# Sixteen conditioning slabs of the second layer in the first mixer, one for each attention step

## The reference, cut to what matters

```
for li in range(DEPTH):
    mod = c_act @ w_ada[li] + b_ada[li]            # (1, 6 * 1024); mod_c likewise from c_ctx
    sh1, sc1, g1, sh2, sc2, g2 = jnp.split(mod, 6)
    m = unpack(modulate(rms_norm(x, norm1_w[li]), sh1, sc1) @ w_in[li], ...)
    att, rec, four = attention(m), gated_recurrence(m), fourier_mix(m)
    x = x + g1 * (concat(att, rec, four) @ w_out[li])
    x = x + g2 * conv_ffn(modulate(rms_norm(x, norm2_w[li]), sh2, sc2), w_up[li], ..., w_down[li])
```

## Time and profile before

| | us |
|---|---|
| median of 3 runs | 1996.9 |
| lowest, highest | 1995.39, 1999.26 |
| the profiled execution, its span | 1989.8 |
| TensorE matmul, busy | 1816.6 (91%) |
| TensorE weight load, busy | 1524.2 (77%) |
| VectorE, busy | 1081.2 (54%) |
| ScalarE, busy | 849.0 (43%) |

### The profile page before, as it was taken

The page is one execution under the profiler, slowest core; times in us unless marked ns, Lnnn a source line. Parts: engine busy times, 40 slices in busy tenths (PEclk is TensorE's granted clock), DMA queues, the critical chain, the costliest instruction groups (busy, mean ns, idle before and its releaser), DMA issues.

```text
span 1989.8 us, 27657 instructions
## 1 busy us (share of the span) xinstructions
PE 1816.6 (91%) x11308; PEld 1524.2 (77%) x11308; DVE 1081.2 (54%) x1620; ACT 849.0 (43%) x1243; POOL 78.0 (4%) x135
## 2 busy tenths in 40 slices
PE   5999888699999999988988889897999899999888
PEld 3777766577777778876766679877999788988776
DVE  1333477654444464454467658755665655545564
ACT  2342444433333343244344445544343446556542
POOL 0000001210000000010001100001000000000010
PEclk9999989899999999988988889898999999999889
DMA  9653200034455532243210455444666455555541
GB/s 292 218 188 114 79 1 1 1 106 153 154 161 168 169 106 96 75 153 128 85 43 1 132 190 189 148 169 127 191 186 183 163 164 169 169 170 169 133 65 43
DMA packets 211596, 261.34 MB, mean 131 GB/s; under 512 B 4673, under 2 KB 173299, under 8 KB 211215
## 3 DMA queue, kind: packets, MB, share of 16 engines
q1 hardware_dynamic: 207850, 248.28, 38.4%
q0 software_dynamic: 3232, 11.15, 3.0%
q10 hardware_dynamic: 389, 0.15, 0.0%
HBM read 258.43 MB, written 1.12 MB: 130 GB/s over the span
## 4 chain that ended last, share of the span: by engine, by line
PE 74%; DVE 10%; ACT 6%; DMA 5%; issue 3%; SPq 1%; POOL 1%; DVEq 0%; ACTq 0%
PE acc L675 21%; PE acc L677 20%; PE acc L676 20%; DVE weights_low L1822 2%; DMA weights<-in_w_in_dram 2%; PE acc L716 2%; DVE scratch L2009 2%; ACT weights_high L1382 2%; PE acc L928 1%; PE acc L1215 1%; DMA weights<-in_w_up_dram 1%; PE acc L1191 1%; PE acc L1145 1%; SPq L1233 1%; DMA weights<-in_w_down_dram 1%
## 5 line engine op out<-in xcount | busy, mean ns | idle before, releaser
L1822 DVE TENSOR_TENSOR weights_low<-weights,weights_high 128x2048 fp32r<-128x2048 f32 (+1 forms) x184 | 416.8, 2268 | 578.0 <-ACT weights_high L1382 577.8
L1382 ACT ACTIVATE weights_high<-weights 128x2048 fp32r<-128x2048 f32 (+1 forms) x184 | 348.3, 1896 | 644.2 <-DMA weights<-in_w_up_dram 190.7
L675 PE MATMUL acc<-normed_t_high,weights_high 128*128 128x256 f32 (+1 forms) x1824 | 580.9, 318 | 12.8 <-DVE weights_low L1822 11.4
L676 PE MATMUL acc<-normed_t_low,weights_high 128*128 128x256 f32 (+1 forms) x1824 | 567.0, 311 | 0.0
L677 PE MATMUL acc<-normed_t_high,weights_low 128*128 128x256 f32 (+1 forms) x1824 | 566.6, 311 | 0.0
L675 PEld LDWEIGHTS acc<-normed_t_high,weights_high 128*128 128x128 f32 x1824 | 348.7, 191 | 41.2 <-DVE weights_low L1822 14.0
L676 PEld LDWEIGHTS acc<-normed_t_low,weights_high 128*128 128x128 f32 x1824 | 346.6, 190 | 24.0 <-issue 4.3
L677 PEld LDWEIGHTS acc<-normed_t_high,weights_low 128*128 128x128 f32 x1824 | 346.0, 190 | 21.3
L675 PE MATMUL acc<-weights_high,normed_t_high 128*128 128x512 f32 (+1 forms) x792 | 314.6, 397 | 33.2 <-DVE normed_t_low L2178 28.3
L676 PE MATMUL acc<-weights_low,normed_t_high 128*128 128x512 f32 (+1 forms) x792 | 310.0, 391 | 0.0
L677 PE MATMUL acc<-weights_high,normed_t_low 128*128 128x512 f32 (+1 forms) x792 | 309.9, 391 | 0.0
(11 more groups left out here) (235 smaller groups left out, 1846.9 us busy)
## 6 DMA issues: line engine op xcount, KB each, us to landing
weights<-in_w_up_dram SPq DMA_DIRECT2D x44, 1024.0 KB, 7.2
weights<-in_attn_w_in_dram SPq DMA_DIRECT2D x40, 1024.0 KB, 5.1
weights<-in_w_ada_dram SPq DMA_DIRECT2D x38, 1024.0 KB, 5.4
weights<-in_conv_w_in_dram SPq DMA_DIRECT2D x32, 1024.0 KB, 5.7
weights<-in_w_in_dram SPq DMA_DIRECT2D x24, 1024.0 KB, 7.3
weights<-in_w_down_dram SPq DMA_DIRECT2D x20, 1024.0 KB, 5.0
arena<-in_w_ada_dram SPq DMA_DIRECT2D x8, 1024.0 KB, 9.9
weights<-in_w_out_dram SPq DMA_DIRECT2D x8, 1024.0 KB, 5.0
```

The lines of the kernel that those rows point to most:

```text
L675: pe.matmul(o, ah, bh, start=start, stop=False)
L676: pe.matmul(o, ah, bl, start=False, stop=False)
L1382: act.activation(hi_slot(n)[:, 0:used], slot(n)[:, 0:used], ACT.Copy).then_inc(hi_in.sem, 1)
L1822: dve.tensor_tensor(slot(n, ring_lo)[:, 0:used], slot(n)[:, 0:used], hi_slot(n)[:, 0:used], ALU.subtract).then_inc(lo_in.sem, 1)
```

## The change

Sixteen slabs of layer 1 leave the `w_up` stage of layer 0 and form a stage ("mixer", 0), one for each of the attention steps 0 to 15. In `plan` they stand between `w_in` and `w_out`. They use one row buffer, `mixer_row`; it was the home of the squares of the head norm, which go to the high slot of the first `w_out` item in layer 0 (`squares_to`). That item is therefore no longer split before the mixer: `split_to` in `w_in` ends one item earlier, and a `split_next` is written at step U + 2 = 18 of ScalarE's `attention` and of VectorE's `combine`. The hunks in order: names, `FILL` and its readers, `row_of`, `plan`, `squares_to`, TensorE's `attention`, ScalarE's `w_in` and `attention`, VectorE's `w_in` and `combine`.

```diff
--- before.py
+++ after.py
@@ -276,6 +276,7 @@
         AT = arena[:, 6144:7168].rearrange("p (b n) -> p b n", b=2)
         ON = ht_r[:, 3080:3336].rearrange("p (b n) -> p b n", b=2)
         o_squares = ht_r[:, 3336:3592].rearrange("p (b n) -> p b n", b=2)
+        mixer_row = ht_r[:, 3336:3592]
         wo_t = scr[:, 0:1024].rearrange("p (b n) -> p b n", b=2)
         START_HOME = [*(arena[:, SLOT * n:SLOT * (n + 1)] for n in range(6)), ht_b[:, 0:SLOT], ht_b[:, SLOT:2 * SLOT]]
         EXTRA = {(0, 18): 4, (0, 19): 8}
@@ -472,13 +473,14 @@
 
         FILL = {"start": ([(0, n) for n in range(8)], [1] * 8),
                 ("w_in", 0): ([(0, n) for n in range(8, 18)], [1] * 10),
-                ("w_up", 0): ([(0, n) for n in range(20, 24)] + [(1, n) for n in (*range(8), *range(12, 20))], [1] * 20),
+                ("mixer", 0): ([(1, n) for n in (*range(8), *range(12, 20))], [1] * 16),
+                ("w_up", 0): ([(0, n) for n in range(20, 24)], [1] * 4),
                 ("w_in", 1): ([(1, n) for n in range(8, 12)], [0, 0, 1, 1, 1, 1]),
                 ("w_up", 1): ([(1, n) for n in range(20, 24)], [1] * 4)}
 
         def fill(stage, n):
 
-            slots, each = FILL[stage]
+            slots, each = FILL.get(stage, ([], []))
             return slots[sum(each[:n]):sum(each[:n + 1])]
 
         def spread(stage, lj):
@@ -488,8 +490,8 @@
 
         def last_spread(stage, n):
 
-            slots, each = FILL[stage]
-            return slots[-1:] if n == len(each) - 1 else []
+            slots, each = FILL.get(stage, ([], []))
+            return slots[-1:] if each and n == len(each) - 1 else []
 
         def first_item(N):
 
@@ -503,6 +505,8 @@
 
             if (li, n) in FILL["start"][0]:
                 return start_rows[:, n, :]
+            if (li, n) in FILL["mixer", 0][0]:
+                return mixer_row
             return extra_rows[:, n % 2, :] if (li, n) in EXTRA else grow[:, ADA_NO[li, n] % 2, :]
 
         def plan_ada(li, n):
@@ -519,6 +523,9 @@
                 else:
                     by_columns(("w_in", li, name, h), W, c0)
                 for lj in fill(("w_in", li), n):
+                    plan_ada(*lj)
+            for n in range(len(att_units(li))):
+                for lj in fill(("mixer", li), n):
                     plan_ada(*lj)
             for c in range(2):
                 for h in range(2):
@@ -573,6 +580,10 @@
 
         def hi_slot(n):
             return ring_hi[:, nth_split[n] % HIGH * SLOT:(nth_split[n] % HIGH + 1) * SLOT]
+
+        def squares_to(li, u):
+
+            return hi_slot(item[("w_out", li, 0, 0)])[:, u % 2 * P:(u % 2 + 1) * P] if li == 0 else o_squares[:, u % 2, :]
 
         def gate_part(li, m):
 
@@ -1000,6 +1011,12 @@
                             r = slice(64 * c, 64 * c + 64)
                             pe.matmul(o[:, 0:nk_], QA[r, h, cols_of(t)], KA[r, h, 0:nk_], start=True, stop=True).then_inc(full, 1)
                     yield
+                    for lj in last_spread(("mixer", li), st - 1):
+                        ada_spread(*lj)
+                    for lj in fill(("mixer", li), st):
+                        for before in spread(("mixer", li), lj):
+                            ada_spread(*before)
+                        ada(*lj)
                     if 0 <= st - 1 < U:
                         u = st - 1
                         t, h = au[u]
@@ -1499,7 +1516,7 @@
                     for lj, at_ in EXTRA.items():
                         if li == 0 and n == at_:
                             ada(*lj)
-                    split_to(min(last_item(("w_in", li, name, h), ("w_in", li), n) + SLOTS, item[("w_out", li, 0, 0)] + 2 - 2))
+                    split_to(min(last_item(("w_in", li, name, h), ("w_in", li), n) + SLOTS, item[("w_out", li, 0, 0)] - (li == 0)))
                 act.wait_ge(full, full_after(("qh", li, 1)))
                 gate_exp(li, 0)
                 gate_high(li, 0)
@@ -1630,7 +1647,7 @@
                         b = slice(u % 2, u % 2 + 1)
                         if u >= 2:
                             act.wait_ge(o_rs.sem, o_rs.after((li, u - 2)))
-                        act.activation(o_squares[:, u % 2, :], bank(("av", li, u), P), ACT.Square,
+                        act.activation(squares_to(li, u), bank(("av", li, u), P), ACT.Square,
                                        scale=arec[:, u % 3, 0:1], accum_out=ossq[:, b]).then_inc(o_sq.sem, 1)
                         act.activation(ON[:, u % 2, :], bank(("av", li, u), P), ACT.Copy, scale=arec[:, u % 3, 0:1]).then_inc(taken_of(("av", li, u)), 1)
                     if 0 <= st - 3 < U:
@@ -1639,6 +1656,11 @@
                         act.wait_ge(full, full_after(("oT", li, u)))
                         act.activation(MT[:, h, cols_of(t)], bank(("oT", li, u), P), ACT.Copy,
                                                            scale=pcol(("subln", li))).then_inc(taken_of(("oT", li, u)), 1)
+                    for lj in fill(("mixer", li), st):
+                        ada(*lj)
+                    if li == 0 and st == U + 2:
+                        act.wait_ge(o_rs.sem, o_rs.after((li, U - 1)))
+                        split_next()
                     yield
 
             def split_rows(X, key, n, r0, nrow, lo, last_read=None):
@@ -2129,6 +2151,13 @@
                         dve.wait_ge(*taken_after(("av", li, u)))
                         dve.tensor_scalar(ON[:, b, :], ON[:, b, :], orstd[:, b:b + 1],
                                                               1.0 - lam_init, ALU.mult, ALU.mult).then_inc(o_done.sem, 1)
+                    for lj in fill(("mixer", li), st):
+                        for before in spread(("mixer", li), lj):
+                            ada(*before)
+                    for lj in last_spread(("mixer", li), st - 1):
+                        ada(*lj)
+                    if li == 0 and st == U + 2:
+                        split_next()
                     yield
 
             def attention(li):
```

## The result

Before: 1996.9 us (median of 7 runs, 1988.1 to 2002.7). After: **2011.6 us** (7 runs, 2005.1 to 2024.1). The ratio is **1.0079**, 95% interval 1.0055 to 1.0104: slower by 11 to 21 us. The forecast was 2008.2, range 1997.5 to 2015.5, with 0.76 for slower. The profiled execution of after has a span of 2007.9 us, against 1989.8: 18.1 us more.

The account below looks back on a forecast made before the run. TensorE bounds the up-projection; the mixer is a ring of small steps around VectorE. Removal -26.2, mixer +18.5, split +7.0, lag +8.5, clock +3.5 sum to +11.3 us, giving 2008.2 us, range 1997.5 to 2015.5.

Parts of the forecast that it names:

- The removal: First up-projection: taking out the sixteen slabs and their spreads saves 26.2 us, all on the path.
- The mixer: First mixer: the slabs moved into its ring of small steps lengthen it by 18.5 us.
- The tail: Mixer steps 14 to 18: the slabs find TensorE idle there and cost 1 us.
- the even steps: Mixer: scores wait for a bank until VectorE's late addition of the spread, delaying the mask; 9.2 us.
- the odd steps: Mixer units 1 to 7: slab ahead of aT delays TensorE's chain to the next s; 8.3 us together.
- The split: First w_out item: VectorE splits it only after the mixer, so TensorE's first w_out matmul comes 7.0 us later.
- The lag: Start of w_up: VectorE stays one split behind, so the first w_up item is split after the norm; 8.5 us later.
- the clock: After the idle gaps before w_out and w_up TensorE restarts at a lower clock; 1.1 and 2.4, together 3.5 us.
- The gaps take it all: Rival: TensorE's idle time in the mixer absorbs the slabs, mixer grows by 3 us; 1992.7 us, chance 0.12.
- The clock stays up: Rival: slabs keep TensorE at 2.4 GHz in the mixer, saving some 5 us; 2003.2 us, chance 0.17.
- The ring pays more: Rival: slabs cost the mixer the upper bound of 28 us instead of 18.5; 2017.7 us, chance 0.14.
- The split does run: Rival: VectorE's w_out split runs inside the mixer, first gap 1.5 us, second none; 1990.7 us, chance 0.03.

Follow-up runs that it names:

- (8): Two kernels against the kernel before: eight slabs in odd or even mixer steps only, eight left in the up-projection, early w_out split; odd 0.9973, even 1.0024.
- the kernel with the lag alone: Kernel before, no slab moved, VectorE's list of splits ending one item earlier in the first w_in; ratio to the kernel before 1.0109, 21.7 us more.
- run 14: Not a label of a run: the text says that from 415.70 to 421.71 us 14 matmuls run, with run as a verb.
- experiment 4: Changed kernel with VectorE's addition of a spread put first in its even combine steps; ratio to the kernel before 1.0067, 2.4 us less than the changed kernel.
- experiment 1: Changed kernel with VectorE's missing first w_out split put right behind the weave; ratio to the kernel before 1.0000, 15.8 us less than the changed kernel.
- the kernel with both edits: Changed kernel with VectorE's w_out split behind the weave and its spread addition first in even steps; ratio to the kernel before 0.9933, then 0.9958.

## Why the forecast held, step by step

**The removal** (-26.2): right, a little low; the kernel without slabs takes 27.2 us less there. The gate spread of slab (0, 23), for which I had kept back 1.0 us, is still there (eight matmuls of L727 at 500.10 us), so some other part of that sum is 1.0 us too low; which is open.

**The mixer** (+18.5, and 1.4 of the split's 7.0 ahead of the rows, together 19.9): the profile shows +23.9. The mean of more executions is nearer to the forecast. The first mask of unit 7 is at 353.40, 355.42 and 360.81 in three executions of the old ring (mean 356.5), and at 373.48, 372.67, 368.62 and 379.77 in four with sixteen slabs and the addition last (mean 373.6): **+17.1** up to there, against 17.5 forecast. The tail from that mask to the rows grew from 31.3 to 35.1, 3.8 us against 1 and 1.4: too small by 1.4. So the sum was right while its split was not: the even steps pay some three times what the odd steps do (8), not 9.2 against 8.3, and that the two misses cancel is luck. In the even steps the bank that waits for the addition is there, 1.45 us in the step shown, as priced. What the price left out is the slab at the low clock: TensorE multiplies it ahead of aT and av, and ScalarE's squares and GpSimd's root come after av. In the kernel with even slabs only VectorE's scale waits 2.45, 2.77 and 2.82 us for the root where the granted clock was 0.72 (264 to 268), 0.50 (284 to 290) and 0.61 (345 to 349), and 0.72 us in the other even steps, as in every even step before. In the odd steps I took the whole slab as delay of s, and gave as its sign 1 to 1.5 us of VectorE's idle time before each maximum. One such step of the kernel after, VectorE's scale, TensorE's s and spread, and VectorE's maximum:

```profile
323.73 0.29 DVE L2152 TENSOR_SCALAR mixer_scratch<-mixer_scratch,small 128x128 f32<-128x128 f32 x1 [0.72 <-POOL small L1298]
...
324.39 1.13 PE L1012 MATMUL acc<-arena 64*128 64x512 f32 x4
325.45 0.61 PE L742 MATMUL acc<-wide_consts,mixer_scratch 128*128 128x2 f32 x4
325.62 1.29 DVE L2175 TENSOR_REDUCE small<-acc 128x1 f32<-128x512 f32 x2 [0.49 <-PE acc L1012]
```

The maximum waits 0.49 us, for 0.18 in the earlier trace rows; over the mixer such waits are 2.7 us in four, for 0.8 in two before, so that sign did not come. A part shows up elsewhere, ahead of the maximum. The scale, which did not wait in this step before,

```profile
312.74 0.28 DVE L2130 TENSOR_SCALAR mixer_scratch<-mixer_scratch,small 128x128 f32<-128x128 f32 x1
```

now waits for GpSimd's root. Up to unit 7 the changed kernel has such a wait in five odd steps, 5.0 us in all (1.75, 0.44, 0.72, 1.34, 0.72), the kernel before in none, that with odd slabs only in the same five (5.0 us), and that with even slabs only in none. So av and the root behind it carry the delay of the odd steps more than s does; what each step had of slack was not measured by itself.

**The split** (7.0 less the 1.4, 5.6): +5.7 in the profile, +5.7 in the kernel with the lag alone. **The lag** (8.5) **and the clock** (1.1 and 2.4): between `w_out` and `w_up` 9.7 for 9.6. But the six kernels with sixteen moved slabs and the split made in time take 56.5 to 57.2 us there, 0.7 to 1.4 more than before, so the gap itself is worth 8.3 to 9.1, and why the rest stays is open. Of the first restart: from 415.70 to 421.71 run 14 matmuls, 6.01 us for 3.24 at 0.2316 each, 2.8 lost for the 1.3 of before, +1.5 for 1.1. In the up-projection the changed kernel is 2.4 us longer than the kernel without slabs (257.53 and 255.16), the 2.4 forecast for the second restart; the same six kernels, without the gap, take 255.14 to 255.17, and the one of experiment 4, with it, 257.57. That row of the clock (0.57 over 476 to 488) also holds TensorE's idle time, so the 2.4 is the difference, not the row. These terms were read out of the code and one row each; experiment 1 takes them back and gives 15.8 us for the 14 to 17 expected (some 22 by its second measurement, 0.9968).

**What was left over**: +3.6 us in the rest of the program, where nothing was changed. The other executions show 1264 to 1276 us there, so it is within the scatter.

**The rivals.** (1) *The gaps take it all*: the mixer would have grown by 3 us; it grew by 17 to 24. The Trainium skill, page Perfetto Trace Analysis, section Optimization Strategy, advises to interleave regimes whose most contended engine differs. The traces say what that takes here: with one bank freed in time and one split in its place the move does pay (0.9933 and 0.9958), as the first change did not. (2) *The clock stays up*: the granted clock over the mixer is 0.89 after and 0.90 before, so the slabs did not lift it as a rule. But in one execution of the kernel with both edits it was 1.00 from 256 to 296, and that one was the fastest profile of all that make the slabs, 1973.4. The Trainium skill, page TensorE: Matmul & The Clock Gate, section What's actually happening, has activity lift the clock. By that rule idle time should go with the low clock; here 36.96 us of busy time in 40 went with 0.70 and 34.95 with 1.00. Busy time is itself longer at the low clock (289 matmuls ended in the one, 357 in the other), but in the 8 us ahead of the fall, 248 to 256, TensorE was busy 5.34 us in the execution that fell and 5.45 in the one that did not. The earlier trace rows had shown it too: 0.50 over 296 to 300, with TensorE busy 4.00 of 4.00 us. What decides is not shown. (3) *The ring pays more*, 28 us: no. (4) *The split does run*: no, by the three splits in a row.

The forecast lay 3.4 us under the measured median, 0.17%.

## What to carry to other kernels

When work is moved between loops that share a list of side jobs (splits, loads), check that each consumer of the list still takes its turn at every place: here a call in a body that a scheduler never reached cost 16 us, as much as the whole change. Idle time of an engine inside a ring of small steps is not room; what a moved piece costs there is decided by the buffers it frees late and by the chain it stands ahead of, so put the release ahead of a wait for another engine, not behind it. And compare a stage over several executions before sizing a term from it: the same mixer differed by up to 12 us.

## What the runs showed that I had not expected

The clock's low stretches inside the mixer move from one execution to the next of the same code: 0.70 or 1.00 over 256 to 296 us (1.00 is 2.4 GHz, 0.50 is 1.2), worth 11.9 us at the mixer's end. TensorE was about 90% busy there in both. And five slabs in the mixer's tail, where TensorE idles (8.76 us busy over 368 to 384 before), cost some 0.5 us each; what ate their gain stood elsewhere, a split ahead of the rows and a spread that waited in the up-projection.
